# An attention and SwiGLU block on one core: gain by matmul, low parts ahead of the maximum, and the first product's pieces spread over all steps

## The reference

```python
h = rms_norm(x, norm_mix_g)
proj = h @ w_in                       # queries, six kinds of keys/values, gates
q = rms_norm(q, q_g); k_sel, k_win = rms_norm(..., k_g)
k_cmp, v_cmp = gelu(blocks(kv) @ w1 + b1) @ w2
out = g0 * softmax(q k_cmp) v_cmp + g1 * softmax(q k_sel) v_sel + g2 * softmax(q k_win) v_win
x = x + out @ w_out
h = rms_norm(x, norm_ffn_g)
x = x + (silu(h @ w_gate) * (h @ w_up)) @ w_down
```

## Time and profile before

| | |
|---|---|
| median of the runs | 2353.47 us |
| profiled execution, its own time | 2356.6 us |
| its span, first to last instruction | 2354.8 us |
| TensorE busy | 2297.0 us (98%), 11955 matmuls |
| VectorE, ScalarE, POOL busy | 1300.9 us, 769.4 us, 76.2 us |
| TensorE's waits for others, all | 53.3 us |
| mean granted TensorE clock | 0.992 |
| chain that ended last, by engine | PE 74%, issue 20%, DVE 4% |

### The profile page before, as it was taken

How to read it: one execution, slowest core, us unless ns; L and a number is a source line. 1 busy time by engine, 2 the same in 40 slices (tenths; PEclk the granted TensorE clock), 3 DMA queues, 4 the chain that set the end, 5 groups by cost and what they waited for, 6 DMA issues and landing times.

```text
span 2354.8 us, 31831 instructions
## 1 busy us (share of the span) xinstructions
PE 2297.0 (98%) x11955; PEld 1969.1 (84%) x11955; DVE 1300.9 (55%) x1987; ACT 769.4 (33%) x1147; POOL 76.2 (3%) x88
## 2 busy tenths in 40 slices
PE   6999999999999999999999999999999999999998
PEld 6898888888889989888888888888888888888886
DVE  5333465665665455456464656556464655564647
ACT  4332344443443233323222322223232322222322
POOL 1000000000000000000000000000000000000000
PEclk9999999999999999999999999999999999999999
DMA  5343211212114122245354453545343525353434
GB/s 173 117 115 92 63 55 55 63 55 60 53 60 143 64 72 73 81 144 152 107 143 127 117 143 107 146 114 143 109 136 106 151 90 152 98 152 117 125 108 134
DMA packets 225613, 254.06 MB, mean 108 GB/s; under 512 B 14187, under 2 KB 188288, under 8 KB 224176
## 3 DMA queue, kind: packets, MB, share of 16 engines
q1 hardware_dynamic: 218192, 223.40, 30.4%
q0 software_dynamic: 7264, 28.51, 6.2%
HBM read 224.59 MB, written 4.19 MB: 97 GB/s over the span
## 4 chain that ended last, share of the span: by engine, by line
PE 74%; issue 20%; DVE 4%; POOL 1%; DMA 1%; ACT 1%; SPq 0%; DVEq 0%; POOLq 0%; ACTq 0%
PE ps L1210 73%; DVE wl L724 1%; DVE x_rows L1143 1%; POOL rqn L400 0%; DMA x_rows<-in_x_dram 0%; DVE ffn_work L1165 0%; DVE ffn_work L1168 0%; DVE x_rows L738 0%; PE ps L1504 0%; PE ps L1540 0%; DVE hTl L724 0%; DMA down<-in_ffn_w_down_dram 0%; POOL krr L400 0%; DVE ffn_work L1174 0%; DVE x_rows L923 0%
## 5 line engine op out<-in xcount | busy, mean ns | idle before, releaser
L1210 PE MATMUL ps<-hTh,wh 128*128 128x512 f32 (+1 forms) x1968 | 766.7, 390 | 9.8 <-DVE wl L724 3.5
L1210 PE MATMUL ps<-hTh,wl 128*128 128x512 f32 (+1 forms) x1968 | 761.0, 387 | 0.0
L1210 PE MATMUL ps<-hTl,wh 128*128 128x512 f32 (+1 forms) x1968 | 760.7, 387 | 0.0
L724 DVE TENSOR_TENSOR wl<-raw,wh 128x1024 fp32r<-128x1024 f32 x298 | 363.0, 1221 | 348.3 <-ACT wh L439 347.9
L439 ACT ACTIVATE wh<-raw 128x1024 fp32r<-128x1024 f32 x298 | 314.4, 1059 | 556.4 <-PE ps L1210 444.0
L1210 PEld LDWEIGHTS ps<-hTh,wh 128*128 128x128 f32 x1968 | 370.9, 188 | 88.3 <-DVE x_rows L1143 5.7
L1210 PEld LDWEIGHTS ps<-hTh,wl 128*128 128x128 f32 x1968 | 370.7, 188 | 75.5
L1210 PEld LDWEIGHTS ps<-hTl,wh 128*128 128x128 f32 x1968 | 371.0, 189 | 72.1
L724 DVE TENSOR_TENSOR wl<-down,wh 128x1024 fp32r<-128x1024 f32 x132 | 161.4, 1223 | 157.5 <-ACT wh L439 157.5
L1210 PE MATMUL ps<-wh,opsh 128*128 128x512 f32 x616 | 241.1, 391 | 6.2 <-DVE opsl L724 3.8
L1210 PE MATMUL ps<-wl,opsh 128*128 128x512 f32 x616 | 240.8, 391 | 0.0
(11 more groups left out here) (173 smaller groups left out, 1995.5 us busy)
## 6 DMA issues: line engine op xcount, KB each, us to landing
raw<-in_ffn_w_gate_dram SPq DMA_DIRECT2D x176, 256.0 KB, 3.0
raw<-in_ffn_w_up_dram SPq DMA_DIRECT2D x176, 256.0 KB, 3.0
down<-in_ffn_w_down_dram SPq DMA_DIRECT2D x176, 256.0 KB, 3.3
raw<-in_nsa_w_in_dram SPq DMA_DIRECT2D x164, 256.0 KB, 3.0
raw<-in_nsa_w_out_dram SPq DMA_DIRECT2D x64, 256.0 KB, 3.1
t<-in_ffn_w_down_dram SPq DMA_DIRECT2D x44, 256.0 KB, 3.3
down<-down POOLq DMA_DIRECT2D x22, 512.0 KB, 5.9
t<-down POOLq DMA_DIRECT2D x22, 512.0 KB, 6.2
```

The lines of the kernel that those rows point to most:

```text
L724: nc.vector.tensor_tensor(dst, src, hi.bitcast(f32), ALU.subtract).then_inc(done, 1)
L1210: return nc.tensor.matmul(out_, a, b, start=start, stop=stop, skip_group_check=True)
```

## The change

- The gain is loaded as one row of 8 KB; TensorE multiplies it with a column of ones into banks 4 to 7, and VectorE copies it to `gain_row`. x tiles 0 and 1 go ahead of the weights, tiles 2 and 3 behind units 0 and 1. The orders on ScalarE, VectorE and TensorE in the start change with it, and TensorE waits there for single quarters of the low parts.
- In the attention's `weigh` the wait for the scores goes (but for i = 0) and stands in `pt_part`, which comes ahead of `maximum`. This holds in the loop and in the last group.
- `FILL_A` has 1, 2, 2, 1 halves over four steps where it had 2, 2, 2, 0. The own low part comes one iteration later (j % 8 = 1).
- At g7 and g15 the two differences move out of the block behind the multiplications and stand behind the first operand's low part. For the last unit of the last slab tile 2 is multiplied and copied as soon as the unit's first half ends.
- Both loops of TensorE are aligned to 256 bytes.

```diff
-FILL_A = [[4, 5], []] + [[h + 6 * c for h in half] for c in range(6) for half in ([6, 7], [8, 9], [10, 11], [])] \
-    + [[42], [43], [], [], [44], [45]]
+FILL_A = [[4], [5]] + [[h + 6 * c for h in half] for c in range(6) for half in ([6], [7, 8], [9, 10], [11])] \
+    + [[42], [], [43], [44], [], [45]]
...
-            for t in range(TT):
+            def x_tile(t):
                 sp.dma_start(x_rows[:, t, :], x[0, t * P:(t + 1) * P, :]).then_inc(x_loaded[t], 16)
-                if t == 0:
-                    sp.dma_start(gain_row[:, :], mix_g.to_broadcast([P, D])).then_inc(gain_loaded, 16)
+
+            sp.dma_start(gain_line[:, :], mix_g).then_inc(gain_loaded, 16)
+            x_tile(0)
+            x_tile(1)
...
                         unit(n, k_halves(n, w_in_v[q][:, :, c:c + 256], 4))
+                        if n < 2:
+                            x_tile(2 + n)
...
+            pool.memset(ones[:, :], 1.0).then_inc(ones_ready, 1)
...
             hidden_columns(0)
+            split(0)
             hidden_columns(1)
-            split(0)
             sum_squares(2)
             split(1)
             sum_squares(3)
+            split(2)
             hidden_columns(2)
-            split(2)
...
+                            if (s, 8 * b + 7) == LAST_UNIT:
+                                act.wait_ge(m_tile, 1)
+                                copy(opsh[:, b, M0A, :], ffn_work[:, 2, 0:256]).then_inc(m_hi, 1)
...
+            for c in range(4):
+                dve.wait_ge(gain_banks, c + 1)
+                nc.vector.tensor_copy(gain_row[:, c * 512:(c + 1) * 512], bank(4 + c)).then_inc(gain_ready, 1)
             norm(0)
             norm(1)
             hidden_columns(0)
-            hidden_columns(1)
+            hidden_columns(1, [0])
             split(0)
+            hidden_columns(1, [1])
+            split(1)
+            hidden_columns(1, [2, 3])
             norm(2)
-            split(1)
+            split(2)
             norm(3)
             hidden_columns(2)
-            split(2)
             hidden_columns(3)
...
-                    if i + 1 < STEPS:
-                        wait(dve, s_done, i + 2, STEPS, g)
+                    if i == 0:
+                        wait(dve, s_done, 2, STEPS, g)
...
                 def pt_part(i):
                     wait(dve, pt_hi, i + 1, STEPS, g)
+                    if i + 2 < STEPS:
+                        wait(dve, s_done, i + 3, STEPS, g)
...
                     if i <= STEPS:
                         weigh(i - 1)
+                    if i >= 2:
+                        pt_part(i - 2)
                     if i < STEPS:
                         maximum(i)
...
                         compressed_thrice(i // 8 + 1)
-                    if i >= 2:
-                        pt_part(i - 2)
...
-                    if last and j >= 8 and j % 8 == 0:
+                    if last and j >= 8 and j % 8 == 1:
...
+                        if (s, j) == LAST_UNIT:
+                            dve.wait_ge(tile_done, 1)
+                            own.done(nc.vector.tensor_tensor(ffn_work[:, 2, :], ps[:, 6, :], rbc[:, :], ALU.mult))
...
-                        own.done(nc.vector.tensor_tensor(s1, m0b, m1b, ALU.subtract))
-                        nc.vector.tensor_tensor(s3, m0a, m0b, ALU.subtract)
...
+                            wait(dve, m_ready, 2 * s + b + 1, 4, i)
+                            own.done(nc.vector.tensor_tensor(s1, m0b, m1b, ALU.subtract))
+                            own.done(nc.vector.tensor_tensor(s3, m0a, m0b, ALU.subtract))
...
+            pe.wait_ge(ones_ready, 1)
+            pe.wait_ge(gain_loaded, 16)
+            for c in range(4):
+                mm(bank(4 + c), ones[:, :], gain_line[:, c * 512:(c + 1) * 512], True, True).then_inc(gain_banks, 1)
+            pe.wait_ge(consts_ready, 1)
             hidden_columns(0)
+            pe.wait_ge(gain_ready, 4)
             hidden_columns(1)
+            for n in range(2):
+                pe.wait_ge(hT_lo, 5 + n)
+                first_unit(n, 0)
+            hidden_columns(2)
             pe.wait_ge(hT_lo, 8)
-            first_unit(0, 0)
-            hidden_columns(2)
-            first_unit(1, 0)
+            first_unit(2, 0)
             hidden_columns(3)
-            first_unit(2, 0)
+            for n in range(3):
+                pe.wait_ge(hT_lo, 13 + n)
+                first_unit(n, 1)
...
+            pe.addr_align(256)
             with pe.Fori(0, LAST) as g:
```

More of the change, by code:

```diff
@@ L112, in nsa_swiglu_block @@
         gain_row = over("gain_row", [P, D], stage_at)
+        ones, gain_line = over("ones", [1, P], q_at + 20 * 1024), over("gain_line", [1, D], q_at + 24 * 1024)
         ffn_work = over("ffn_work", [P, 4, S], stage_at)
@@ L1163, in slab @@
                     if kind == "g" and j in (7, 15):
+                        if (s, j) == LAST_UNIT:
+                            dve.wait_ge(tile_done, 1)
+                            own.done(nc.vector.tensor_tensor(ffn_work[:, 2, :], ps[:, 6, :], rbc[:, :], ALU.mult))
+                            own.settle()
+                            dve.wait_ge(silu_done, 2 * s + 2)
+                            nc.vector.tensor_tensor(ffn_work[:, 2, :], ffn_work[:, 0, :], ffn_work[:, 2, :], ALU.mult)\
+                                .then_inc(m_tile, 1)
+                            dve.wait_ge(m_hi, 6 * s + 4)
+                            lo(opsl[:, 1, M0A, :], ffn_work[:, 2, 0:256], opsh[:, 1, M0A, :], m_lo)
+                            tiles, rows = slice(3, 4), rbc[:, :].rearrange("p (a c) -> p a c", a=1)
+                        else:
+                            tiles, rows = slice(2, 4), both
@@ L1164, in slab @@
                         wait(dve, units_used, n + 1, 2 * TURN, i)
-                        own.done(nc.vector.tensor_tensor(ffn_work[:, 2:4, :], ps[:, 4 * b + 2:4 * b + 4, :], both, ALU.mult))
+                        own.done(nc.vector.tensor_tensor(ffn_work[:, tiles, :],
+                                                         ps[:, 4 * b + tiles.start:4 * b + 4, :], rows, ALU.mult))
                         own.settle()
                         wait(dve, silu_done, 2 * s + b + 1, 4, i)
-                        nc.vector.tensor_tensor(ffn_work[:, 2:4, :], ffn_work[:, 0:2, :], ffn_work[:, 2:4, :], ALU.mult)\
-                            .then_inc(m_ready, 1)
@@ L1170, in slab @@
-                        wait(dve, m_ready, 2 * s + b + 1, 4, i)
-                        m0a, m0b, m1a, m1b = (ffn_work[:, 2 + c, a:a + 256] for c in range(2) for a in (0, 256))
-                        s1, s2, s3, n4 = (ffn_work[:, c, a:a + 256] for c in range(2) for a in (0, 256))
-                        own.done(nc.vector.tensor_tensor(s1, m0b, m1b, ALU.subtract))
-                        nc.vector.tensor_tensor(s3, m0a, m0b, ALU.subtract)
+                        nc.vector.tensor_tensor(ffn_work[:, tiles, :], ffn_work[:, tiles.start - 2:2, :],
+                                                ffn_work[:, tiles, :], ALU.mult).then_inc(m_ready, 1)
@@ L1182, in slab @@
-                            own.done(nc.vector.tensor_tensor(s2, s1, m0a, ALU.subtract))
+                            m0a, m0b, m1a, m1b = (ffn_work[:, 2 + c, a:a + 256] for c in range(2) for a in (0, 256))
+                            s1, s2, s3, n4 = (ffn_work[:, c, a:a + 256] for c in range(2) for a in (0, 256))
+                            if (s, 8 * b + 7) != LAST_UNIT:
+                                wait(dve, m_hi, 6 * s + 3 * b + 1, 12, i)
+                                lo(opsl[:, b, M0A, :], m0a, opsh[:, b, M0A, :], m_lo)
@@ L1197, in _ @@
             with dve.Fori(0, PAIRS) as i:
[L1198 removed]
+                own.enter(i, 16)
                 for h in range(2):
@@ L1570, in norm_bcast, with hidden_unit @@
                 last.then_inc(rb_done, 1)
-            def hidden_unit(n, j):
+            def hidden_unit(n, s, j):
                 for half in range(2):
-                    columns_half(n, j % 8 // 2, half, j // 8 * 4 + j % 2 * 2 + half)
+                    last = columns_half(n, j % 8 // 2, half, j // 8 * 4 + j % 2 * 2 + half)
+                    if (s, j) == LAST_UNIT and half == 0:
+                        last.then_inc(tile_done, 1)
             def product(n, j):
```

27 lines of the change are left out of this document (13 added, 14 removed).

## The result

| | before | changed |
|---|---|---|
| median of six runs each, us | 2352.64 | 2361.80 |
| lowest and highest, us | 2351.03, 2353.63 | 2361.25, 2368.06 |
| profiled execution, its own time | 2356.6 | 2361.66 |
| its span | 2354.8 | 2359.6 |

The change makes the kernel slower: the ratio is 1.0043 with a 95% interval from 1.0033 to 1.0053, 9.2 us between the medians where 2.3 us less were forecast. The profiled execution of before lay 4.0 us above the median of its kernel, that of the changed kernel at its median. So the two profiles differ by 4.8 us of span only. The rest of the 9.2 lies between the profile of before and the executions it stands for.

A forecast was written before the change was run, and what follows sets the result against it. TensorE, with 74% of the chain, was taken as the bound, so only its waits and granted clock counted. Terms -4.0 - 0.9 - 0.8 + 10.2 - 5.5 - 1.3 = -2.3 on 2353.47 gave 2351.2 us, range 2344.5 to 2358.5.

The forecast's parts named there:

- the clock term: Last group: four to five partly filled lowered-clock stretches behind seven new waits, less one already there: +4.0 us.
- Base: Sum of changes added to the runs' median, 2353.47 us; the profiled execution's own time was 2356.6.
- Start: Kernel start: x tile 1 arrives earlier, less a cost for the gain's way through TensorE: -4.0 us (-2.5 to -5).
- Loop groups: Three attention loop groups: a scaling wait in step 28 goes, a smaller one comes in 29: -0.9 us (-2 to +1).
- Alignment: Turns of TensorE's attention loop: aligning shortens the stand there, worth between nothing and 2.0 us: -0.8 us.
- Last group: Last attention group: seven new waits for the first product's add, net +6.2, plus clock +4.0: +10.2 us.
- FFN: Ten FFN slabs: unit g8's wait for the sum of d12 goes, 0.55 us each: -5.5 us (0 to -5.5).
- After the last slab: Behind the last FFN slab: tile 2 handled alone lets products 0 and 2 start earlier: -1.3 us (-2.2 to 0).
- Rival (b): Last group, blocks 1 to 7: clock falls at every block, +10.4 instead of +4; 2359.4 us; chance 0.14.

The follow-up runs named there:

- ffn_only: Kernel before with only the two subtractions of an FFN slab moved behind the first operand's low part: 2347.66 us, ratio 0.9982.
- no_last_tile: Changed kernel with split adds, without alignment, and the last slab's last unit treated like all others: 2334.11 us, ratio 0.9917.
- split_adds: Changed kernel with each half's bank added for itself, the first one step earlier: 2338.21 us, ratio 0.9937.
- order_old_last: Changed kernel with VectorE's order of before (scaling waits for scores, maximum, low part) in the last group alone: 2370.50 us, ratio 1.0073.

## Why the prediction was wrong, point by point

Stage by stage, the two profiles are 7.1 us further apart than the sum of -2.3 said. The last group missed by +5.0, all of it the clock term (+4.0 taken, +9 measured). The alignment missed by +3.4: a gain was forecast, and its filling instructions made a stop. The start missed by +1.5 and the end by +0.3; the loop groups (-2.2) and the slabs (-0.8) went the other way. Most of the other 3.5 us is the base of the sum.

- **Base.** The profile of before was 4.0 us above its kernel's median, and I added the sum to a median 3.1 below that profile. The profiles show a change of +4.8, the medians +9.2: the new kernel's sum was made against an execution with four lowered stretches in the loop groups, and its own profile had two there (-3.1 us, which is no effect of the change: ffn_only ran the same code in 442.9). This was in sight: the prediction set down both numbers and didn't ask what the 3 us between them were.
- **Start** (-4.0; marks -2.5, time 0). norm(0) started at 11.40, not 9.2. The second token halves began at 36.70, where 34.9 was forecast. The eight passes of the gain's four matmuls took 0.85 us each (6.8 us, forecast 6.5 as the upper bound). This is twice what the eight in the earlier trace rows come to for 512 columns, and so I take it for the lower clock; the trace's record of the granted clock begins later. But the order on VectorE was misread: the mean stands behind the fourth copy, and root and mean (0.94 us) came on top:

```profile
9.86 0.69 DVE L762 COPY gain_row<-ps 128x512 f32<-128x512 f32 x1 [1.01 <-PE ps L1242]
10.46 0.14 DVE L746 TENSOR_SCALAR rr<-ss 128x1 f32<-128x1 f32 x1
10.69 0.58 POOL L409 TENSOR_TENSOR rr<-rr,neg_half 128x1 f32<-128x1 f32 x1 [3.41 <-DVE rr L746]
...
11.40 2.35 DVE L751 SCALAR_TENSOR_TENSOR x_rows<-x_rows,rr,gain_row 128x2048 f32<-128x2048 f32 x1 [0.79 <-POOL rr L409]
```

- **Loop groups** (-0.9; by the waits +1.1). The waits for the scaling shrank (0.77 for 0.95, 1.04 for 1.13, each counted as what the start came late), and the one in step 28 is gone as forecast, but `values` now waited 0.57 and 0.4 us for the low part, which itself waits for the scores: the cost of the wait was looked for behind it, at the maximum, and not at the tile it writes. The sum per group is 4.5 for 4.6 us. The turns grew by 0.6 and 0.7 us.
- **Alignment** (-0.8; stage +2.6, medians +4.4 to +5.0 with the intervals above). This step was wrong in kind. It was bounded by the turn, from nothing to a gain of 2.0, and what the edit issues, filling instructions, was not counted at all.
- **Last group** (+10.2; +15.2). The waits were right: by starts 2.17, three of 2.58, three of 2.71, together 18.0 us, the forecast's 18.0, and L1021's waits there are gone. So was the net +6.3. The clock was mis-sized: +4.0 taken, +9 measured (six stretches of 1.49, one more at the group's beginning, one less at 731.9). I held that dense work on both sides would protect it; it doesn't. Rival (b) had this, with its condition of six stretches; its 2359.4 took +10.4 for the clock. It deserved more than 0.14.
- **FFN** (-5.5; -6.3 in the profile, 4.6 alone). Right.
- **After the last slab** (-1.3; -1.0 without the slab's share). The operand's wait was 1.7 (forecast 1.9) and a wait of 2.4 us for an add came behind it (forecast 2.6). But no_last_tile shows that little of it comes from the tile.

The parts measured alone don't sum to the whole either: pieces +16.0, order +4.6, start +0.9, slabs -4.6 and alignment +4.4 to +5.0 make 21 us or more, where the whole change cost 9.2. What the clock gives and takes between them stays open.

## What to carry to other kernels

When work is spread to fill empty steps, look at where the last piece on a bank and the first piece of the next now meet: the bank must be emptied piece by piece, each as soon as its own sum ends, or the spreading makes the wait it was to remove. A wait has two prices, its length and what the clock does behind it; at this place of the kernel 1.3 us cost 1.3, and 2.4 cost 3.9 three times in four. But a wait that is short or gone is no promise that the clock stays up elsewhere. Count every instruction that an edit issues, an alignment's filling too, and ask whether the execution profiled is a typical one before its stalls are priced.

## What the runs showed of the hardware

- A taken branch at the turn of TensorE's loop occupies its sequencer for microseconds: in the changed kernel the three of the attention's loop took 3.81, 3.65 and, the last and untaken, 0.08 us; in the FFN's loop the taken ones took 3.3 to 5.2 over all profiles. At the attention's turn TensorE stops 2.45 us after the branch begins (2.9 in the old order of VectorE) and starts again 0.25 to 0.33 us after it ends (390.82, 394.64 and 394.89 in the changed kernel), so the branch ends this wait and not the low queries that the profile names. The FFN's turn mostly shows no wait, some 15 queued matmuls of 512 columns starting meanwhile; but where its branch took 5.2 us (split_adds) and 4.8 (order_old_last) TensorE stood 1.54 and 1.11 us. The Trainium skill (Advanced Engine Details and Errata, Control Flow Timing) gives a compare-and-branch some 108 ns, which the untaken one (83 ns) is near and the taken ones are not.

```profile
L1567 PEldq COMPARE_BRANCH  x3: 83/3647/3814, 390.8 to 690.9; - x3
```

- A do-nothing instruction lasts 13 ns in the trace, but 0.072 us from start to start.
- A full-precision matmul of one row with 512 columns in the start: two passes of 0.85 us.
- Medians of nearly equal kernels differ from their stalls' sum by 2 to 5 us. The executions of one kernel differ by as much (split_adds: 2336.9 to 2345.6), and in the profiles the number of lowered stretches in the loop groups goes from two to six.
